# Gating's first projection as seven quarter products, with weight sums made in HBM and six token sums on GpSimd

## The chip, the cores and the metric

One core of a Trainium2 chip runs the kernel. The metric is the device time of one execution in microseconds (us). The engines are PE (TensorE, matmuls), DVE (VectorE), ACT (ScalarE), POOL (GpSimd) and SP (SyncE, which only issues transfers). Each runs its own instructions in order and waits on semaphores.

## The reference, cut to what matters

Two decoder layers on 512 tokens of width 1024. Layer 0 mixes tokens with a convolution module, layer 1 with spatial gating. After each comes a gated ConvFFN and, after every sublayer, a LayerNorm. The change lies in the gating of layer 1:

```python
z = gelu(x @ w_in + b_in)            # x 512 x 1024, w_in 1024 x 2048
u, v = split(z, 2)                   # 1024 columns each
v = layer_norm(v, ln_g, ln_b)
s = einsum("gts,bnsgc->bntgc", w_causal, v) + b_s   # 4 chunks of 128, 8 groups
y = (u * s) @ w_out + b_out
x = layer_norm(alpha * x + y)
```

All values are float32.

## The kernel before

**Numbers.** Each float32 operand is split into a high part (a copy in the matmul's float type, made by ACT) and a low part (the rest, a subtraction on DVE). A product is three matmuls: high by high, high by low, low by high.

**Weights.** All weights pass as units of 128 x 1024 (512 KB), numbered in order of use. SP loads unit u into slot u mod 4 of `raw` (L532) when the low part of unit u-4 is done (L560). `his` (L761) makes the high part, `los` (L1273) the low part, into rings of 4, some units ahead of PE. The first four units of the gating (U_GV to U_GV+3) go to places of their own, `eh` and `el`. `w_used` counts the units that PE is done with, and `his` waits for it before it overwrites a place.

**Order in time around the change.** The down-projection of the first ConvFFN (`ffn_down` on ACT and DVE, `ffn(0, 1, ...)` on PE) already works by Strassen's method with seven products. Its last one, `fourth` (L2342), ends token block by token block. Each block of 128 tokens is then normed on DVE (`mean_of`, `centred`, `normed`) and transposed on PE (`block_fm`, L2176) into PSUM. ACT copies it to `xh` (`block_hi`, L964), and DVE subtracts it to `xl` (`block_lo`, L1529).

**The v half** (L2388, L2389): `down_by_block(U_GV, ...)` makes columns 0 to 511 for one token block after the other, 24 matmuls each (L2027 to L2029), into banks 4 to 7; `down_by_k(U_GV + 4, ...)` makes columns 512 to 1023, unit by unit for all four blocks, into banks 0 to 3. DVE adds the bias row `gvrow` (L1943) into `vtm`, ACT takes Gelu (L1232), DVE takes statistics (L1948). `residual(2)` (L1544), which scales the residual and adds a bias row, stands on DVE between the two halves.

**The u half** (L2404 to L2413): 8 units, 24 matmuls each (`up`, L2012), each ending in a Gelu on ACT. Beside it DVE norms v (L1962, L1966), splits it and so feeds `spatial` (L2390), four groups of which follow the last two u units. `gated` (L1975) multiplies on DVE. Then the output projection (`down_by_k(U_GOUT, ...)`, L2421) needs `xl` of each group (L1996).

**GpSimd's queue**: for the first ConvFFN it makes the weight sums by transfers that add in HBM (`summed_weights`, L689), from raw copies that SP issues (`copies`, L534). Then come the roots of the norms (`norm_root`, L596), the mask of the spatial weights (L743) and the roots for v.

## Time and profile before

| | before |
|---|---|
| median of 3 runs | 1015.76 us (1015.53 to 1019.26) |
| profiled execution, its own time | 1015.58 us |
| its span, first to last instruction | 1013.8 us |
| share of the span: PE / DVE / ACT / POOL busy | 99% / 86% / 60% / 23% |
| the stage of the change, by PE | 525 to 618 us |

The page of the profile gives each engine's busy time and the groups of instructions. The timeline lists one engine's instructions with start, duration and line, and in brackets how long the engine was idle before it and what ended that. A matmul of 512 columns has a record of 0.39 us, but the next starts 0.23 us later: they are pipelined. The view of waits sums the idle time by what ended it. The view of stretches gives busy time and transfers between two moments.

### The profile page before, as it was taken

The page shows a single profiled execution, that of the slowest core. Times are in us where ns is not written, and L with a number is a line of the kernel's source. Part 1 is how long each engine was busy: PE and PEld are TensorE (multiplying, and loading weights), DVE is VectorE, ACT ScalarE, POOL GpSimd, SP SyncE. Part 2 cuts the span into 40 slices and gives each one's busy share as a digit, 9 for nine tenths or more (in the row PEclk, how much of TensorE's full clock was granted, in tenths as well). Part 3 has the DMA queues.
Part 4 walks back from the last instruction along what each step waited for, and adds up shares of the span by engine and source line. Part 5 has one row for each costly group of instructions (what it writes and reads, how often), then busy time and mean ns, then how long its engine had stood idle before and what let it go on. Part 6 is the DMA issues. An engine that isn't in the chain of part 4 may idle for free.

```text
span 1013.8 us, 15746 instructions
## 1 busy us (share of the span) xinstructions
PE 1003.6 (99%) x5379; PEld 861.1 (85%) x5379; DVE 867.6 (86%) x1228; ACT 604.5 (60%) x903; POOL 233.3 (23%) x289
## 2 busy tenths in 40 slices
PE   9999999999999999999999999999999999999997
PEld 7777788988899988888888888898988999888885
DVE  6999977897988988898894878779888888879888
ACT  7889865564565556666454343457555555566653
POOL 2998730023232121000010210002423212100001
PEclk9999999999999999999999999999999999999999
DMA  9766269369889676376555333825989966627652
GB/s 342 218 161 166 58 147 349 119 196 238 236 211 228 220 169 173 102 271 208 195 179 194 118 111 107 307 79 186 262 237 229 220 209 173 163 98 260 205 197 112
DMA packets 65590, 194.02 MB, mean 191 GB/s; under 512 B 7552, under 2 KB 8576, under 8 KB 65024
## 3 DMA queue, kind: packets, MB, share of 16 engines
q1 hardware_dynamic: 44144, 137.76, 39.1%
q0 software_dynamic: 19376, 48.24, 23.7%
q10 hardware_dynamic: 2016, 7.34, 2.1%
q8 instruction: 28, 0.46, 0.2%
q14 instruction: 26, 0.21, 0.1%
HBM read 178.11 MB, written 54.53 MB: 229 GB/s over the span
## 4 chain that ended last, share of the span: by engine, by line
PE 78%; DVE 5%; DMA 3%; issue 2%; ACT 1%; SPq 0%; DVEq 0%; POOL 0%; POOLq 0%; ACTq 0%
PE ps L2017 10%; PE ps L2018 10%; PE ps L2019 10%; PE ps L2306 6%; PE ps L2307 6%; PE ps L2308 6%; PE ps L2259 5%; PE ps L2260 5%; PE ps L2261 5%; PE ps L2027 4%; PE ps L2028 4%; PE ps L2029 4%; DMA raw<-d_weights 3%; PE ps L2186 1%; DVE ps L1618 1%
## 5 line engine op out<-in xcount | busy, mean ns | idle before, releaser
L2017 PE MATMUL ps<-xh,wh 128*128 128x512 f32 x528 | 208.5, 395 | 0.3 <-DVE wl L1280 0.3
L2018 PE MATMUL ps<-xl,wh 128*128 128x512 f32 x528 | 205.7, 390 | 0.0
L2019 PE MATMUL ps<-xh,wl 128*128 128x512 f32 x528 | 205.6, 389 | 0.0
L767 ACT ACTIVATE wh<-raw 128x1024 fp32r<-128x1024 f32 x114 | 119.9, 1057 | 80.4 <-PE ps L2308 49.5
L1280 DVE TENSOR_TENSOR wl<-raw,wh 128x1024 fp32r<-128x1024 f32 x101 | 123.2, 1224 | 32.9 <-ACT wh L767 32.5
L702 POOL DMA_DIRECT2D summed<-d_weights x88 | 75.2, 1115 | 198.0 <-PE ps L2019 96.4
L2017 PEld LDWEIGHTS ps<-xh,wh 128*128 128x128 f32 x528 | 99.2, 188 | 22.0 <-issue 1.2
L2019 PEld LDWEIGHTS ps<-xh,wl 128*128 128x128 f32 x528 | 99.1, 188 | 21.0
L2018 PEld LDWEIGHTS ps<-xl,wh 128*128 128x128 f32 x528 | 99.2, 188 | 20.7 <-issue 1.2
L2306 PE MATMUL ps<-wh,parts 128*128 128x512 f32 x264 | 102.9, 390 | 0.0
L2308 PE MATMUL ps<-wh,parts 128*128 128x512 f32 x264 | 102.7, 389 | 0.0
L2307 PE MATMUL ps<-wl,parts 128*128 128x512 f32 x264 | 102.7, 389 | 0.0
L1607 DVE TENSOR_TENSOR wl<-raw,wh 128x1024 fp32r<-128x1024 f32 x62 | 75.6, 1220 | 22.5 <-ACT wh L1014 22.5
L599 POOL TENSOR_SCALAR veps<-sqs 128x1 f32<-128x1 f32 x15 | 4.8, 323 | 385.2 <-ACT squares_down L961 266.2
L1376 DVE SCALAR_TENSOR_TENSOR ps<-glu,par,ps 128x512 f32<-128x512 f32 x125 | 84.7, 752 | 0.6 <-PE ps L2103 0.4
L622 POOL TENSOR_TENSOR gsum<-gsum,prods 128x512 f32<-128x512 f32 x53 | 70.2, 1324 | 14.5 <-ACT prods L836 8.4
L1014 ACT ACTIVATE wh<-raw 128x1024 fp32r<-128x1024 f32 x62 | 65.6, 1058 | 8.2 <-DMA raw<-d_weights 8.2
L1618 DVE SCALAR_TENSOR_TENSOR ps<-vpad,par,ps 128x512 f32<-128x512 f32 x80 | 60.3, 753 | 8.0 <-ACT ps L1038 2.2
L1618 DVE SCALAR_TENSOR_TENSOR ps<-gpad,par,ps 128x512 f32<-128x512 f32 x80 | 60.2, 753 | 6.4 <-DVE ps L1618 2.1
L2306 PEld LDWEIGHTS ps<-wh,parts 128*128 128x128 f32 x264 | 49.5, 188 | 11.1 <-DVE wl L1280 0.8
L2308 PEld LDWEIGHTS ps<-wh,parts 128*128 128x128 f32 x264 | 49.5, 188 | 10.4
L2307 PEld LDWEIGHTS ps<-wl,parts 128*128 128x128 f32 x264 | 49.6, 188 | 10.2
(266 smaller groups left out, 2543.9 us busy)
## 6 DMA issues: line engine op xcount, KB each, us to landing
raw<-d_weights SPq DMA_DIRECT2D x156, 512.0 KB, 4.9
raw<-summed SPq DMA_DIRECT2D x56, 512.0 KB, 4.1
summed<-d_weights POOLq DMA_DIRECT2D x88, 256.0 KB, 9.5
summed<-d_weights SPq DMA_DIRECT2D x66, 256.0 KB, 5.2
summed<-summed POOLq DMA_DIRECT2D x46, 256.0 KB, 4.8
res<-brow POOLq DMA_DIRECT2D x12, 512.0 KB, 10.7
wl<-raw POOLq DMA_DIRECT2D x4, 1024.0 KB, 6.9
wl<-raw POOLq DMA_DIRECT2D x5, 512.0 KB, 6.3
```

The lines of the kernel that those rows point to most:

```text
L702: eng.dma_start(out, of, accum_op=ALU.add).then_inc(w_sum[i % AHEAD], 16)
L767: eng.activation(split_at(u)[0], raw[:, u % RAW, :], ACT.Copy).then_inc(w_hi, 1)
L1280: eng.tensor_tensor(l, raw[:, u % RAW, :], h.bitcast(f32), ALU.subtract).then_inc(w_lo, 1)
L1376: eng.scalar_tensor_tensor(out=ps[:, bank, :], in0=glu[:, j % 2, k:k + SEQ], scalar=par[:, c:c + 1], in1=ps[:, bank, :], op0=ALU.mult, op1 ...
L1607: eng.tensor_tensor(wl[:, slot, :], raw[:, part, :], wh[:, slot, :].bitcast(f32), ALU.subtract).then_inc(w_lo, 1)
L1618: eng.scalar_tensor_tensor(out=accs[v], in0=buf[:, off:off + SEQ], scalar=par[:, bass.ds(cw, 1)], in1=accs[v], op0=ALU.mult, op1=ALU.add). ...
L2017: eng.matmul(ps[:, bank, cols], a, xh[:, k, cols], start=(k == 0), stop=False)
L2018: eng.matmul(ps[:, bank, cols], a, xl[:, k, cols], start=False, stop=False)
L2019: mm = eng.matmul(ps[:, bank, cols], b, xh[:, k, cols], start=False, stop=(k == KD - 1))
L2306: eng.matmul(ps[:, bank + t, :], s_h, w_h[:, cols], start=first, stop=False)
L2307: eng.matmul(ps[:, bank + t, :], s_h, w_l[:, cols], start=False, stop=False)
L2308: mm = eng.matmul(ps[:, bank + t, :], s_l, w_h[:, cols], start=False, stop=last)
```

## The change

The v half is made by Strassen's method (Winograd's form). The tokens and the input channels are cut in two each (A11, A12, A22 and so on), and so are the weights. Seven products of quarter size: P1 and P2 straight from x, a fourth (`g22`) with a weight sum, then one u unit (U_GU0), the fifth and sixth (`U_G56`), the third and seventh (`U_G37`), and the other seven u units. Six more units pass through the loads and the splits (GV_MORE).

- Weight sums: SP copies raw parts into `gsum_d` at units 22 to 25 of the first up-projection; GpSimd's queue adds to them behind `up_sums(0)`; SP waits for the sums before it loads U_GV+4.
- Token sums: ACT keeps copies of three token quarters (`block_kept`, `second_kept`), DVE makes `gn5` and `gs2`, GpSimd makes `gs4` and `gv7`, each for two token blocks. ACT and DVE split them (`token_hi`, `token_lo`).
- Outputs: DVE reads each product from PSUM and adds or subtracts it in `vtm`. GpSimd makes two of these sums (with `both_rows`, a sum of two bias rows, ahead).
- `residual(2)` moves behind the norm of v. Row transfers of ACT move.

The host puts the v weights into units whose halves are W11 | W21 and W12 | W22. The diff, cut:

```diff
+GQ = KD // 2
+U_GU0 = U_GV + GQ + 2
+U_G56 = U_GU0 + 1
+U_G37 = U_G56 + GQ
+U_GU = U_G37 + GQ - 1
 U_GOUT = U_GU + KD
+GV_MORE = 6
...
+        def gv_copies(i):
+
+            w1, w2 = weights_d[raw_gv + i], weights_d[raw_gv + GQ + i]
+            eng.dma_start(gsum_d[2 + i, :, 0:HALF], w1[:, 0:HALF]).then_inc(gv_copied, 16)
+            eng.dma_start(gsum_d[2 + GQ + i, :, HALF:UNIT], w2[:, 0:HALF]).then_inc(gv_copied, 16)
+            eng.dma_start(gsum_d[2 + GQ + i, :, 0:HALF], w2[:, HALF:UNIT]).then_inc(gv_copied, 16)
 
         for k in range(KD):
...
+                eng.wait_ge(gv_sum, 16 * (4 + 2 * GQ))
             load(u % RAW, u)
+            if 0 <= u - U_UP0 - 2 * KQ < GQ:
+                gv_copies(u - U_UP0 - 2 * KQ)
             for layer in range(DEPTH):
...
+        w1, w2 = weights_d[raw_gv:raw_gv + GQ], weights_d[raw_gv + GQ:raw_gv + 2 * GQ]
+        fifth, third = gsum_d[2:2 + GQ], gsum_d[2 + GQ:2 + 2 * GQ]
+        eng.wait_ge(gv_copied, 16 * 3 * GQ)
+        eng.dma_start(fifth[:, :, first], w2[:, :, first], accum_op=ALU.add).then_inc(gv_sum, 16)
+        eng.dma_start(third[:, :, second], w2[:, :, second], accum_op=ALU.add).then_inc(gv_sum, 16)
+        eng.wait_ge(gv_sum, 16 * 2)
+        eng.dma_start(fifth[:, :, second], fifth[:, :, first]).then_inc(gv_sum, 16)
+        eng.wait_ge(gv_sum, 16 * 3)
+        eng.dma_start(fifth[:, :, second], w2[:, :, second], accum_op=ALU.add).then_inc(gv_sum, 16)
+        eng.wait_ge(gv_sum, 16 * 4)
+        for i in range(GQ):
+            eng.dma_start(gsum_d[i // 2, :, second if i % 2 else first], fifth[i, :, second]).then_inc(gv_sum, 16)
+        eng.wait_ge(gv_sum, 16 * (4 + GQ))
+        for i in range(GQ):
+            eng.dma_start(gsum_d[i // 2, :, second if i % 2 else first], w1[i, :, second], accum_op=ALU.add).then_inc(gv_sum, 16)
         for t in range(NT):
             norm_root(ROOTS + NT + t, NT + t + 1, t)
+        eng.wait_ge(gv_in, 16)
+        eng.wait_ge(w_used, U_GV)
+        eng.tensor_tensor(both_rows[:, :], gvrow[:, 0:HALF], gvrow[:, HALF:D], ALU.add).then_inc(rows_ok, 1)
+        eng.wait_ge(rows_ok, 1)
+        for t in range(NT // 2):
+            eng.wait_ge(gv_rd, t + 1)
+            eng.tensor_tensor(vtm[:, 2 + t, HALF:D], vtm[:, 2 + t, 0:HALF], both_rows[:, :], ALU.subtract).then_inc(n_ok, 1)
+        eng.wait_ge(w_used, U_GV + GQ)
+        eng.wait_ge(x_kept, 2 * NT)
+        for t in range(NT // 2):
+            cols = slice(t * P, (t + 1) * P)
+            eng.wait_ge(ga_sum, 2 * t + 2)
+            eng.wait_ge(a22_kept, t + 1)
+            eng.tensor_tensor(gs4[:, :, cols], gs2[:, :, cols], a12f[:, :, cols], ALU.add).then_inc(ga_more, 1)
+            eng.tensor_tensor(gv7[:, :, cols], gs2[:, :, cols], a22f[:, :, cols], ALU.add).then_inc(ga_more, 1)
 
...
                 his([U_GV + 2, U_GV + 3])
+                block_kept(n, 0, 0)
+                block_kept(n, 0, 1)
...
+                his([U_GV + GQ, U_GV + GQ + 1])
                 squared(n, 3)
-                for t in (2, 3):
-                    block_hi(n, t, 0)
-                    block_hi(n, t, 1)
+                block_hi(n, 2, 0)
+                block_hi(n, 2, 1)
+                block_kept(n, 1, 0)
+                block_kept(n, 1, 1)
+                second_kept(0)
+                block_hi(n, 3, 0)
+                block_hi(n, 3, 1)
+                his([U_GU0])
+                second_kept(1)
 
         norm(0)
...
-                eng.activation(vtm[:, t, h * HALF:(h + 1) * HALF], vtm[:, t, h * HALF:(h + 1) * HALF], ACT.Gelu).then_inc(v_gelu, 1)
-                if h == 0:
-                    his([U_GV + 4 + t])
-            if h == 0:
-                row(glb[:, :], R_GLB, gm_in)
-                his(range(U_GU, U_GU + LEAD))
-        his([U_GU + LEAD])
+        token_hi(gn5h, gn5, 0, ga_sum, 1)
+        token_hi(gs2h, gs2, 0, ga_sum, 2)
+        his([U_G56])
+        token_hi(gn5h, gn5, 1, ga_sum, 3)
+        token_hi(gs2h, gs2, 1, ga_sum, 4)
+        his([U_G56 + 1])
+        gelu_v(0, 0, G_C11 - 1)
+        gelu_v(1, 0, G_C11)
+        row(glb[:, :], R_GLB, gm_in)
+        his([U_G56 + 2])
+        gelu_u(0)
+        his([U_G56 + 3])
+        for t in range(NT // 2):
+            token_hi(gs4h, gs4, t, ga_more, 2 * t + 1)
+            token_hi(gv7h, gv7, t, ga_more, 2 * t + 2)
+        his([U_G37, U_G37 + 1])
+        eng.wait_ge(w_used, U_G37)
+        row(glg[:, :], R_GLG, gm_in)
+        eng.dma_start(wsraw[:, :, :], spatial_d).then_inc(gm_in, 16)
+        his([U_G37 + 2, U_G37 + 3, unit_gu(1)])
+        gelu_v(0, 1, G_C12 - 1)
+        gelu_v(1, 1, G_C12)
+        his([unit_gu(2)])
+        for h, last in ((1, G_C22), (0, G_C21)):
+            for t in range(NT // 2):
+                gelu_v(2 + t, h, last - 1 + t)
+        his([unit_gu(3), unit_gu(4)])
         eng.wait_ge(ws_m, 1)
...
+
+        def gv_first(t):
+
+            eng.wait_ge(gv_pe, t + 1)
+            eng.tensor_tensor(vtm[:, 2 + t, 0:HALF], ps[:, 4 + t, :], gvrow[:, 0:HALF], ALU.add).then_inc(gv_rd, 1)
...
             normed(n, 3)
+            gv_first(1)
             block_lo(n, 2)
+            los([U_GV + GQ, U_GV + GQ + 1])
             block_lo(n, 3)
 
         first_halves(0, U_CONV_OUT + 4)
...
 
-        eng.wait_ge(gv_in, 16)
-        for h in range(2):
-            for t in range(NT):
-                if h == 0 and t < NT - 1:
-                    eng.wait_ge(blk, blk_gv + t + 1)
-                else:
-                    eng.wait_ge(w_used, U_GV + 4 * (h + 1))
-                cols = slice(h * HALF, (h + 1) * HALF)
-                eng.tensor_tensor(vtm[:, t, cols], ps[:, 4 - 4 * h + t, :], gvrow[:, cols], ALU.add).then_inc(v_ev, 1)
-                if h == 0:
...
-            if h == 0:
-                los([U_GU])
-                residual(2)
-                los([U_GU + 1, U_GU + 2])
-        los([U_GU + LEAD])
+        def token_lo(to, of, high, t, count):
+
+            cols = slice(t * P, (t + 1) * P)
+            eng.wait_ge(ga_hi, count)
+            eng.tensor_tensor(to[:, :, cols], of[:, :, cols], high[:, :, cols].bitcast(f32), ALU.subtract).then_inc(ga_lo, 1)
+
+        def gv_stat(t, h, count):
+
+            eng.wait_ge(v_gelu, count)
+            return stat(eng.bn_stats(stats[:, t, h, :], vtm[:, t, h * HALF:(h + 1) * HALF]))
...
+        eng.wait_ge(w_used, U_GV + GQ)
+        for t in halves:
+            eng.wait_ge(gv_rd, t + 1)
+            eng.tensor_tensor(vtm[:, t, c1], ps[:, 6 + t, :], vtm[:, 2 + t, c1], ALU.add).then_inc(gv_rd, 1)
+        los([U_GU0])
+        eng.wait_ge(x_kept, 2 * NT)
+        for t in halves:
+            cols = slice(t * P, (t + 1) * P)
+            eng.wait_ge(a22_kept, t + 1)
+            eng.tensor_tensor(gn5[:, :, cols], ps[:, B0[1] + 2 * t, :].rearrange("p (k n) -> p k n", k=4), a22f[:, :, cols],
+                              ALU.subtract).then_inc(ga_sum, 1)
+            eng.wait_ge(ga_sum, 2 * t + 1)
+            eng.tensor_tensor(gs2[:, :, cols], gn5[:, :, cols], a11f[:, :, cols], ALU.subtract).then_inc(ga_sum, 1)
+        eng.wait_ge(ga_sum, 4)
+        token_lo(gn5l, gn5, gn5h, 0, 1)
+        token_lo(gs2l, gs2, gs2h, 0, 2)
+        los([U_G56])
+        los([U_G56 + 1])
+        token_lo(gn5l, gn5, gn5h, 1, 3)
+        token_lo(gs2l, gs2, gs2h, 1, 4)
+        los([U_G56 + 2])
+        eng.wait_ge(w_used, U_GU0)
+        eng.wait_ge(n_ok, NT // 2)
+        for t in halves:
+            eng.tensor_tensor(vtm[:, 2 + t, c1], ps[:, 4 + t, :], vtm[:, 2 + t, c1], ALU.add).then_inc(gv_rd, 1)
+        los([U_G56 + 3])
+        for t in halves:
+            token_lo(gs4l, gs4, gs4h, t, 4 + 2 * t + 1)
+            token_lo(gv7l, gv7, gv7h, t, 4 + 2 * t + 2)
+        los([U_G37, U_G37 + 1])
+        eng.wait_ge(w_used, U_G37)
+        for t in halves:
+            eng.wait_ge(gv_rd, G_MP4)
+            eng.tensor_tensor(vtm[:, 2 + t, c1], ps[:, 2 + t, :], vtm[:, 2 + t, c1], ALU.add).then_inc(gv_rd, 1)
+        for t in halves:
+            eng.tensor_tensor(vtm[:, 2 + t, c2], ps[:, 2 + t, :], vtm[:, 2 + t, c2], ALU.add).then_inc(gv_rd, 1)
+        los([U_G37 + 2, U_G37 + 3])
+        for t in halves:
+            eng.wait_ge(gv_rd, G_NP6 - 1 + t)
+            eng.tensor_tensor(vtm[:, 2 + t, c2], vtm[:, 2 + t, c2], ps[:, t, :], ALU.subtract).then_inc(gv_rd, 1)
+        gv_stat(0, 0, 1)
+        gv_stat(1, 0, 2)
+        los([unit_gu(1)])
+        eng.wait_ge(gv_pe, 3)
+        for t in halves:
+            eng.wait_ge(gv_rd, G_NP5 - 1 + t)
+            eng.tensor_tensor(vtm[:, t, c2], ps[:, 6 + t, :], vtm[:, 2 + t, c2], ALU.subtract).then_inc(gv_rd, 1)
+        eng.wait_ge(w_used, U_GU + 1)
+        for t in halves:
+            eng.wait_ge(gv_rd, G_C12 - 1 + t)
+            eng.tensor_tensor(vtm[:, 2 + t, c2], ps[:, 4 + t, :], vtm[:, 2 + t, c2], ALU.subtract).then_inc(gv_rd, 1)
+        for t in halves:
+            eng.tensor_tensor(vtm[:, 2 + t, c1], vtm[:, 2 + t, c1], ps[:, 4 + t, :], ALU.subtract).then_inc(gv_rd, 1)
+        los([unit_gu(2)])
+        gv_stat(0, 1, 3)
+        gv_stat(1, 1, 4)
+        gv_stat(2, 1, 5)
+        gv_stat(3, 1, 6)
+        gv_stat(2, 0, 7)
+        n = gv_stat(3, 0, 8)
+        los([unit_gu(3)])
         eng.wait_ge(st_ok, n)
...
+
+        residual(2)
 
         def gated(g):
...
-                block_fm(1, 2 + t)
-        down_by_block(U_GV, 4, 4, xh, xl, 0, KD, last_block, lambda t: wait_x(1, t))
-        down_by_k(U_GV + 4, 4, 0, xh, xl, 0, KD)
+        g11, g12, g22 = [[x[:, k, t] for x in (xh, xl)] for k, t in
+                         ((slice(0, GQ), slice(0, HQ)), (slice(GQ, KD), slice(0, HQ)), (slice(GQ, KD), slice(HQ, SEQ)))]
+        gn5p, gs2p, gs4p, gv7p = (gn5h, gn5l), (gs2h, gs2l), (gs4h, gs4l), (gv7h, gv7l)
+
+        def gv(u, c, bank, tokens, i, t):
+
+            h, l = split_at(u)
+            w_h, w_l = h[:, c * HALF:(c + 1) * HALF], l[:, c * HALF:(c + 1) * HALF]
+            s_h, s_l = [x[:, i, t * P:(t + 1) * P] for x in tokens]
+            eng.matmul(ps[:, bank + t, :], s_h, w_h, start=(i == 0), stop=False)
+            eng.matmul(ps[:, bank + t, :], s_h, w_l, start=False, stop=False)
+            return eng.matmul(ps[:, bank + t, :], s_l, w_h, start=False, stop=(i == GQ - 1))
+
+        for t in range(NT // 2):
+            wait_x(1, t)
+            for i in range(GQ):
+                if t == 0:
+                    eng.wait_ge(*lo_of(U_GV + i))
+                mm = gv(U_GV + i, 0, 4, g11, i, t)
+            mm.then_inc(gv_pe, 1)
+            eng.wait_ge(c_rd, R_P4 + 1 + t)
+            for i in range(GQ):
+                mm = gv(U_GV + i, 1, 6, g12, i, t)
+                if t == 1:
+                    mm.then_inc(w_used, 1)
+            block_fm(1, 2 + t)
+        eng.wait_ge(gv_rd, G_M)
+        for t in range(NT // 2):
+            wait_x(1, 2 + t)
+            for i in range(GQ):
+                u = U_GV + GQ + i // 2
+                if t == 0 and i % 2 == 0:
+                    eng.wait_ge(*lo_of(u))
+                mm = gv(u, i % 2, 4, g22, i, t)
+                if t == 1 and i % 2:
+                    mm.then_inc(w_used, 1)
+        eng.wait_ge(*lo_of(U_GU0))
+        eng.wait_ge(gv_rd, G_C11)
+        up(split_at(U_GU0), GU_BANK[0]).then_inc(w_used, 1)
+        for pair in range(GQ // 2):
+            for t in range(NT // 2):
+                eng.wait_ge(ga_lo, 2 * t + 2)
+                for i in (2 * pair, 2 * pair + 1):
+                    u = U_G56 + i
+                    if t == 0:
+                        eng.wait_ge(*lo_of(u))
+                    gv(u, 0, 0, gn5p, i, t)
+                    mm = gv(u, 1, 2, gs2p, i, t)
+                    if t == 1:
+                        mm.then_inc(w_used, 1)
+
+        def gv_third(i):
+            eng.wait_ge(*lo_of(U_G37 + i))
+            for t in range(NT // 2):
+                mm = gv(U_G37 + i, 0, 6, gs4p, i, t)
+            if i == GQ - 1:
+                mm.then_inc(gv_pe, 1)
+
+        def gv_seventh(i):
+            for t in range(NT // 2):
+                mm = gv(U_G37 + i, 1, 4, gv7p, i, t)
+            mm.then_inc(w_used, 1)
+
+        eng.wait_ge(ga_lo, 8)
+        eng.wait_ge(u_gelu, 1)
+        eng.wait_ge(gv_rd, G_MP4)
+        for i in range(GQ):
+            gv_third(i)
+            if i < GQ - 2:
+                gv_seventh(i)
+        gv_seventh(GQ - 2)
+        gv_seventh(GQ - 1)
 
         def spatial(g):
...
 
-        for j in range(KD):
+        for j in range(1, KD):
             eng.wait_ge(*lo_of(U_GU + j))
-            if j < 4:
-                eng.wait_ge(v_ev, j + 1)
-            else:
-                eng.wait_ge(u_gelu, j - 3)
-            up(split_at(U_GU + j), 4 + j % 4).then_inc(w_used, 1)
+            if j == 1:
+                eng.wait_ge(gv_rd, G_NP5)
+            if j == 5:
+                eng.wait_ge(gv_rd, G_C21)
+            up(split_at(U_GU + j), GU_BANK[j]).then_inc(w_used, 1)
             if j >= KD - 2:
...
     weights = np.ascontiguousarray(np.concatenate(units))
 
```

## Rows read from the trace of the kernel before

**Rows 1.** The page, part 1: busy us (share of the span) xinstructions.

```profile
PE 1003.6 (99%) x5379; PEld 861.1 (85%) x5379; DVE 867.6 (86%) x1228; ACT 604.5 (60%) x903; POOL 233.3 (23%) x289
```

**Rows 2.** Waits of PE, whole span: us in total, times, longest.

```profile
PE ps L2146 <- POOL ident L606: 1.6, 1, 1.6
PE ps L2259 <- DVE wl L1684: 0.8, 1, 0.8
```

**Rows 3.** Timeline of PE: start us, us, engine, line, operation.

```profile
525.06 0.48 PE L2027 MATMUL ps<-eh,xh 128*128 128x512 f32 x1
...
537.90 0.47 PE L2027 MATMUL ps<-eh,xh 128*128 128x512 f32 x1
...
570.64 0.39 PE L2017 MATMUL ps<-xh,wh 128*128 128x512 f32 x1
...
617.84 0.45 PE L2027 MATMUL ps<-wh,xh 128*128 128x512 f32 x1
```

**Rows 4.** Stretches: us, busy us (instructions) per engine, granted clock, DMA share, GB/s.

```profile
525.06:570.64 45.58, 45.58 (x211) 37.71 (x210) 29.95 (x36) 16.21 (x22) 4.16 (x5) 1.00 0.55 187
```

**Rows 5.** Groups by line: operation, shapes, count, busy us, mean ns, idle before.

```profile
L767 ACT ACTIVATE wh<-raw 128x1024 fp32r<-128x1024 f32 x114 | 119.9, 1057 | 80.4 <-PE ps L2308 49.5
L1280 DVE TENSOR_TENSOR wl<-raw,wh 128x1024 fp32r<-128x1024 f32 x101 | 123.2, 1224 | 32.9 <-ACT wh L767 32.5
L1376 DVE SCALAR_TENSOR_TENSOR ps<-glu,par,ps 128x512 f32<-128x512 f32 x125 | 84.7, 752 | 0.6 <-PE ps L2103 0.4
L622 POOL TENSOR_TENSOR gsum<-gsum,prods 128x512 f32<-128x512 f32 x53 | 70.2, 1324 | 14.5 <-ACT prods L836 8.4
...
L1800 DVE TENSOR_TENSOR parts<-made,parts 128x512 fp32r<-128x512 f32 x50 | 32.5, 687 | 0.0
```

**Rows 6.** Timelines of DVE and POOL, 527 to 536 us.

```profile
527.03 1.22 DVE L1280 TENSOR_TENSOR el<-raw,eh 128x1024 fp32r<-128x1024 f32 x1
...
533.79 1.29 DVE L1772 SCALAR_TENSOR_TENSOR res<-scaled_down,rstd,brow_n 128x1024 f32<-128x1024 f32 x1 [0.89 <-POOL rstd L588]
534.99 1.28 DVE L1532 TENSOR_TENSOR xl<-ps,xh 128x512 fp32r<-128x512 f32 x2
...
533.14 0.54 POOL L588 TENSOR_TENSOR rstd<-veps,half_m 128x1 f32<-128x1 f32 x1
```

**Rows 7.** DVE beside POOL: timelines, and L1548's durations (min/median/max ns).

```profile
559.55 1.68 POOL L743 TENSOR_SCALAR_AFFINE_SELECT wsraw<-wsraw 128x1024 f32<-128x1024 f32 x1 [25.87 <-DMA glb<-d_rows]
...
L1548 DVE SCALAR_TENSOR_TENSOR res<-res,brow x4: 1214/1214/2124, 560.2 to 564.5; 128x1024 f32<-128x1024 f32 x4
...
106.11 7.01 POOL L622 TENSOR_TENSOR gsum<-gsum,prods 128x512 f32<-128x512 f32 x5 [2.08 <-ACT prods L836]
...
112.44 1.24 DVE L1321 TENSOR_TENSOR glul<-glu,gluh 128x512 fp32r<-128x512 f32 x1
...
580.90 1.22 DVE L1280 TENSOR_TENSOR wl<-raw,wh 128x1024 fp32r<-128x1024 f32 x1
...
581.38 0.81 POOL L593 TENSOR_SCALAR veps<-mv 128x1 f32<-128x1 f32 x1
```

**Rows 8.** Timeline of DVE, 577 to 614 us.

```profile
577.90 1.27 DVE L1962 SCALAR_TENSOR_TENSOR vtm<-vtm,mv,glg 128x1024 f32<-128x1024 f32 x1
...
597.86 1.23 DVE L1970 TENSOR_TENSOR vl<-vtm,vh 128x1024 fp32r<-128x1024 f32 x1
...
609.79 0.69 DVE L1982 TENSOR_TENSOR vtm<-ps,bsrow 128x512 f32<-128x512 f32 x1 [3.34 <-PE ps L2401]
...
613.92 1.22 DVE L1280 TENSOR_TENSOR wl<-raw,wh 128x1024 fp32r<-128x1024 f32 x1
```

**Rows 9.** Transfers: a stretch, ACT's timeline, ACT's waits between 150 and 250 us.

```profile
290.00:300.00 10.00, 10.00 (x51) 8.51 (x51) 8.81 (x14) 5.19 (x9) 2.46 (x3) 1.00 1.06 261
...
289.51 1.06 ACT L1014 ACTIVATE wh<-raw 128x1024 fp32r<-128x1024 f32 x1 [1.88 <-DMA raw<-d_weights]
...
ACT wh L1014 <- DMA raw<-d_weights: 4.5, 1, 4.5
```

100 lines of the change are left out of this document (67 added, 33 removed).

## Prediction

> **What bounds the kernel now.** I read the page first: TensorE (PE) is busy for 99% of the span [rows 1]. Then the waits of PE: the longest anywhere is 1.6 us, and there is none in the stage that is changed [rows 2]. So today every microsecond of matmul work is on the path, and work of the other engines costs only when it makes PE wait. Next the timeline of PE in the stage. The first projection (the v half) starts at 525.06, its third token block at 537.90, the other half (u) at 570.64, and the output projection at 617.84 [rows 3]. Between 537.90 and 570.64 lie 2 x 24 + 4 x 24 = 144 matmuls, so one takes 32.74 / 144 = 0.227 us. Last, the stretch 525.06 to 570.64 by engine: VectorE (DVE) is busy for 30.0 of 45.6 us, ScalarE (ACT) for 16.2, GpSimd (POOL) for 4.2, PE's granted clock is 1.00 [rows 4]. DVE has 15.6 us free there. I take the change to be a trade: less work on PE for more on DVE and POOL, and ask at each step what is late.
>
> **Removed.** Strassen computes the v half with seven quarter products in place of eight: 7 x 24 = 168 matmuls for 192. 24 x 0.227 = **-5.4 us**, and since PE waits for nothing here, all of it counts until another engine is late.
>
> **Added, by count.** Six more weight units, each with a load, a high part on ACT (1.06 us) and a low part on DVE (1.22 us) [rows 5]: 7.3 us of DVE. Eight low parts of token sums and four token sums, each 512 columns at 0.69 [rows 5]: 8.3. Eighteen readings of products where eight were: ten more, 6.9. Together 22.5 us of DVE, for 15.6 free. Part of it goes behind the u units, and `residual(2)` (about 5 us) leaves the stretch. So DVE is full rather than over-full, and the order inside decides. POOL gets seven sums of 1.32 us [rows 5]. ACT gets 6 x 1.06 plus some 14 pieces of 0.6: 15 us, for 29 free; it is nowhere last, and its three row transfers and its Gelu table load lie before waits for DVE. Each order below is walked with these durations; an instruction of 512 columns holds DVE for 0.60, one of 1024 for 1.14 to 1.20, since neighbours overlap a little [rows 6].
>
> **Step A: the first products eat units twice as fast.** P1 takes three matmuls from a unit where a block took six, so it wants the low part of unit U_GV+3 after 9 matmuls: 525.06 + 9 x 0.227 = 527.1. DVE makes it from 527.03 to 528.25, behind two steps of the norm [rows 6]. Before, it was wanted only after 18 matmuls, at 529.1. Nothing in the change moves it. **+1.1 us**, and I hold this for the surest cost. The order then runs to the fourth product at 537.90 + 1.1 = 539.0.
>
> **Step B: GpSimd's first three sums.** Both a VectorE instruction with two SBUF inputs and a GpSimd one seem to need something that only one can have. At 560.2 one of four equal `residual` instructions took 2.12 us where the median is 1.21, beside GpSimd's mask at 559.55 to 561.23. At 112.44 a 512-column subtraction took 1.24 in place of 0.69, beside the last of five GpSimd sums, which ended at 113.12. DVE goes on 0.13 before the GpSimd record ends, in both [rows 7]. The other way, a GpSimd instruction asked at 581.38 and ended at 582.19, right after DVE's 580.90 + 1.22: it slips in between two back-to-back DVE instructions [rows 7]. So I let the two engines take turns, and a GpSimd sum costs a DVE instruction of that kind up to 1.19 us. `both_rows` has no open wait after the root that ends about 533.7, where DVE starts the last `normed` at 533.79 [rows 6]: DVE waits 1.2. One of the next two sums falls beside readings of PSUM, which are free; the other delays the low part of U_GV+4 by 0.7. Add `gv_first` (0.60). The low part ends at 539.8 or so, against 539.0 plus its own hand-over: **+1.0 us**. If GpSimd comes after `normed`, U_GV+5 is late instead, by 0.8.
>
> The Trainium skill, page "SBUF — State Buffer", section "Who interferes with whom", says that a VectorE instruction with two SBUF inputs contends with a GpSimd one that reads SBUF and that the loser is blocked for the whole instruction. By that rule each turn costs 1.32 and not 1.19, and the time below would be 0.8 us more. That it holds at all speaks against giving sums to GpSimd; these rows agree but for the last 0.13.
>
> **Step C: the token sums.** Behind the fourth product's units DVE has two readings, one low part, and then `gn5`, `gs2` twice. The first `gs2` ends at 545.7, and GpSimd starts its four sums at once. The next four DVE instructions with two SBUF inputs (`gs2`, `token_lo` twice, the low part of U_G56) each find it taken: 0.6 + 1.1 + 1.2 + 1.2 = 4.1 us. The low part of U_G56 is done at 553.5. PE has finished u unit 0, put there as a cover, at 539.0 + 1.0 + 48 x 0.227 = 550.7. **+2.9 us.** Without the turns it would be done near 548 and the cover would be enough. After that DVE keeps 0.5 to 2 us ahead to the end of the seventh product, though each unit's low part is wanted every 1.4 to 2.7 us.
>
> **Step D: behind the product.** Four readings, a low part, six statistics and another low part follow PE's last matmul: the norm of v starts 8.8 us after it. Today 577.90 - 570.64 = 7.3. The norm takes 597.86 - 577.90 = 20.0 [rows 8] and 1.1 for its last piece. Before, 3.3 us of idle lay ahead of `gated(0)` and more before that [rows 8]. Now `residual(2)` stands there: 4 x 1.20 = 4.8. Then two low parts 2.3, `gated(0)` and `gated(1)` 613.92 - 609.79 = 4.1, a low part 1.1, the first `xl` 0.7. Sum 8.8 + 20.0 + 1.1 + 4.8 + 2.3 + 4.1 + 1.1 + 0.7 = 42.9. PE needs 7 x 24 x 0.227 = 38.1 and 4 spatial groups of 0.9: 41.7. **+1.2 us.** Were `residual(2)` free, PE would be last.
>
> **Step E: transfers.** Twelve copies of 256 KB stand on SP's queue in the first up-projection, and GpSimd issues sums of 1 MB parts after `up_sums(0)`, far ahead of their use (about 100 us). The loads behind the copies land later. ACT waited 1.9 us for one at 289.51 and up to 4.5 us for one earlier, with no wait of PE beside either [rows 9, 2]. I put this at **0**, hidden by the three units that the split runs ahead; the bounds are in the rivals. It could not be below nothing.
>
> **Sum.** -5.4 + 1.1 + 1.0 + 2.9 + 1.2 = +0.8. The profiled execution took 1015.58 us (span 1013.8), within 0.2 of the median of 1015.76. 1015.6 + 0.8 = **1016.4 us**.
>
> **Rivals.**
> 1. The turns do not happen, or GpSimd waits instead of DVE. For: the small GpSimd instruction at 581.38 waited for DVE, not the other way [rows 7], and DVE's 125 taps, with one SBUF input, kept 752 ns beside GpSimd's sums [rows 5]. Against: the two rows of step B, both of this very kind. B and C fall: 1015.6 - 5.4 + 1.1 + 1.2 = 1012.5.
> 2. Slower, by step E. Place: units 22 to 25 of the first up-projection, near 284 to 306 us, where the DMA engines are fully busy (1.06) at 261 GB/s [rows 9]. Price: 0.75 MB per unit is 2.9 us at that rate, 5.7 if read and write both count. It decides from where ACT's wait passes the 4.5 us that stayed hidden: 1.9 + 2.9 = 4.8 is just there, 1.9 + 5.7 = 7.6 costs 3.1 a unit. Two units with such a delay give 1016.4 + 6 = 1022.6; all four 1029. Against: the same copies for the first 11 units cost PE nothing.
> 3. The change does not save its matmuls' time, PE being held at DVE's pace all through: 22.5 us more on DVE with 15.6 free is 6.9 over, less 5 moved away, less 5.4 saved, leaves DVE's idle time of start and end as the only reserve. That gives 1016 to 1018, inside the range.
>
> **Chances.** Forecast with its variants (1014.5 to 1018.5) 0.62; rival 1 0.19; rival 2 0.11; something beyond 0.08. Range: 1012.0 to 1019.0, from rival 1 to the forecast with every turn whole and 2 us of step E. A measurement of this kernel can tell about 0.5%, 5.1 us. The saving is 5.4 at most, and step A alone eats 1.1, so faster by more than that is hardly possible: 0.03. Slower needs 1020.8 or more: 0.11. Same: 0.86.
>
> **What would show it.** In PE's waits: about 1.1 us for the low part of `el` at the first product (A); about 1 us near 539 (B); 2 to 3 us for the first unit of the fifth product near 551 (C); about 1 us at the output projection for `xl` (D). In DVE's timeline: `token_lo` and low parts of 1.3 to 2.4 us beside GpSimd's sums. If all DVE instructions there keep 0.69 and 1.22, rival 1 holds. If PE waits before 420 us, rival 2 does. A new wait elsewhere, above all for a raw unit or for ACT, would make the prediction wrong.

## The result, and the profile after

The changed kernel takes 1033.76 us (median of 4 runs, 1032.52 to 1039.21), the kernel before 1016.29 in the same comparison. The ratio is 1.018, with a 95% interval of 1.014 to 1.022: slower by about 17 us, where the prediction said no change. The profiled execution took 1032.52 us, with a span of 1030.8.

The page of the changed kernel, part 1, against [rows 1]:

```profile
PE 1002.9 (97%) x5355; PEld 859.2 (83%) x5355; DVE 891.8 (87%) x1256; ACT 617.3 (60%) x923; POOL 253.8 (25%) x308
```

There are 24 matmuls fewer, as the change says. But PE is busy for 97% of the span now, not 99%. Its waits, over the whole span, against [rows 2] (us in total, times, longest):

```profile
PE ps L2443 <- ACT made L1153: 6.9, 2, 5.8
PE ps L2577 <- DVE wl L1401: 2.9, 2, 2.5
PE ps L2443 <- DVE wl L1805: 1.8, 1, 1.8
...
PE ps L2490 <- DVE wl L1401: 1.1, 2, 0.6
PE ps L2577 <- DVE el L1401: 0.9, 1, 0.9
PE ps L2212 <- DVE xl L2181: 0.7, 1, 0.7
```

Two places are to be told apart. L2577 and L2212 are matmuls of the gating stage and of its output projection: the waits of steps A to D. L2443 is in the first up-projection, some 220 us earlier, where no matmul was changed. That is the larger part. The timeline of PE, first at the up-projection and then in the stage (start, us, operation, and in brackets the idle time before it with what ended it):

```profile
308.09 0.39 PE L2443 MATMUL ps<-parts,wh 128*128 128x256 f32 x1 [1.81 <-DVE wl L1805]
310.89 0.39 PE L2443 MATMUL ps<-parts,sum2h 128*128 128x256 f32 x1 [1.10 <-ACT made L1153]
319.75 0.58 PE L2443 MATMUL ps<-xh,parts 128*128 128x256 f32 x1 [5.78 <-ACT made L1153]
...
543.05 0.50 PE L2577 MATMUL ps<-eh,xh 128*128 128x512 f32 x1 [0.92 <-DVE el L1401]
554.41 0.47 PE L2577 MATMUL ps<-wh,xh 128*128 128x512 f32 x1 [0.41 <-DVE wl L1401]
...
632.69 0.47 PE L2212 MATMUL ps<-wh,xh 128*128 128x512 f32 x1 [0.69 <-DVE xl L2181]
```

**Where the 17 us are.** I cut both executions at five matmuls of PE: the first of the first up-projection (`fh`), the first of the down-projection (`wh,parts`), the first of the gating stage (`eh`), the last of the gating output projection (`bh`), and the last of all. The differences of their starts, in us:

| execution | to up | up | down | gating stage | second layer | end | span |
|---|---|---|---|---|---|---|---|
| before | 182.6 | 235.4 | 107.1 | 141.7 | 339.9 | 7.2 | 1013.8 |
| after | 184.9 | 245.9 | 109.1 | 141.8 | 339.8 | 9.3 | 1030.8 |
| difference | +2.3 | +10.5 | +2.0 | +0.1 | 0 | +2.1 | +17.0 |

"End" is from the start of the last matmul to the end of the span. The stage that the change is about came out even: +0.1, where the prediction had +0.8. All the rest lies outside it. The first column differs among all the executions of this study by up to 2.7 us without a pattern. Besides the 1.6 us of [rows 2], PE waits there for 1.3 us for `xh` and 1.2 for `res` in after, but for 0.4 us in all in e4 and 2.3 in e5 (both below), which run the same instructions there as after; so the +2.3 is not put down to the change. The up-projection of the eleven kernels that have none of the copies in it, or only one of them, takes from 234.0 to 236.0 (234.7 in the mean), so differences under 2 us between two executions are not read there.

**The up-projection.** In SP's queue, each of the four loads (L571) is followed by three copies (L584 to L586), and the loads after them come late. SP's timeline at the fourth of them, and ACT's (start, us):

```profile
292.26 0.60 SPq L571 DMA_DIRECT2D raw<-d_weights  x1
292.91 1.40 SPq L584 DMA_DIRECT2D gsum<-d_weights  x1
294.35 3.06 SPq L585 DMA_DIRECT2D gsum<-d_weights  x1
297.45 0.61 SPq L586 DMA_DIRECT2D gsum<-d_weights  x1
...
318.37 1.06 ACT L1101 ACTIVATE wh<-raw 128x1024 fp32r<-128x1024 f32 x1 [6.93 <-DMA raw<-d_weights]
325.43 1.06 ACT L1101 ACTIVATE wh<-raw 128x1024 fp32r<-128x1024 f32 x1 [5.46 <-DMA raw<-d_weights]
```

ACT waits for raw weights, its next instruction (`made`) stands behind that wait, and PE waits for `made`. Of the transfers issued from 250 to 300 us (KB each, median us to landing), the copies take three times as long as the loads:

```profile
raw<-d_weights SPq DMA_DIRECT2D x8, 512.0 KB, 6.4
gsum<-d_weights SPq DMA_DIRECT2D x12, 256.0 KB, 18.9
```

The median hides what happens to the four loads. The first of them, and the fourth, issued at 292.26:

```profile
raw<-d_weights SPq DMA_DIRECT2D x1, 512.0 KB, 5.5
...
raw<-d_weights SPq DMA_DIRECT2D x1, 512.0 KB, 26.0
```

The two between them took 11.1 and 18.8 us: each load, with three copies more ahead of it, takes 5.6 to 7.7 us longer to land than the one before. The fourth lands at 318.3, and with it ACT's wait of 6.93 us ends. In the kernel before the loads issued from 280 to 292 us land after 6.6 to 9.3 us.

And PE does not run at full clock when it comes back. Stretches (length, then busy us and instructions of PE, PEld, DVE, ACT, POOL, then granted clock, DMA share, GB/s):

```profile
315.00:320.00 5.00, 0.25 (x1) 0.25 (x2) 0.54 (x1) 1.60 (x3) 0.81 (x1) 0.80 1.08 250
320.00:325.00 5.00, 5.00 (x25) 5.00 (x26) 1.08 (x2) 0.00 (x0) 0.00 (x0) 0.52 1.06 340
```

PE is busy for 0.25 us from 315 to 320 us, and then works for 5 us at 0.52 of the full clock, the level of 1.2 GHz: some 2.4 us lost (0.48 of 5 us). Waits of 8.7 us, what each hides besides (below, 0.7), 2.4 for the clock, less the 0.8 and 0.2 of before's own wait at this line [rows 2]: 10.8 for 10.5 measured.

### The profile page after: what moved, and what is told of

Same layout as the page of the kernel before. It is cut to its first block, busy times and chain, and to the rows that moved or that the text cites. A ratio compares the mean times of both kernels' runs of the same rounds, so it can differ in the third digit from the quotient of the medians.

```text
span 1030.8 us, 15810 instructions
## 1 busy us (share of the span) xinstructions
PE 1002.9 (97%) x5355; PEld 859.2 (83%) x5355; DVE 891.8 (87%) x1256; ACT 617.3 (60%) x923; POOL 253.8 (25%) x308
## 4 chain that ended last, share of the span: by engine, by line
PE 44%; DVE 7%; issue 2%; DMA 2%; ACT 1%; POOL 0%; DVEq 0%; POOLq 0%; ACTq 0%
PE ps L2202 5%; PE ps L2203 5%; PE ps L2204 5%; PE ps L2490 4%; PE ps L2491 4%; PE ps L2492 4%; PE ps L2444 3%; PE ps L2445 3%; PE ps L2443 3%; DVE wl L1401 2%; PE ps L2212 1%; PE ps L2213 1%; PE ps L2214 1%; DMA raw<-d_weights 1%; DMA raw<-summed 1%
## 5 line engine op out<-in xcount | busy, mean ns | idle before, releaser
L847 ACT ACTIVATE wh<-raw 128x1024 fp32r<-128x1024 f32 x120 | 125.7, 1056 | 84.0 <-PE ps L2492 41.2
L1401 DVE TENSOR_TENSOR wl<-raw,wh 128x1024 fp32r<-128x1024 f32 x107 | 132.3, 1245 | 22.8 <-ACT wh L847 21.8
L1728 DVE TENSOR_TENSOR wl<-raw,wh 128x1024 fp32r<-128x1024 f32 x62 | 75.6, 1220 | 27.1 <-ACT wh L1101 27.0
L1101 ACT ACTIVATE wh<-raw 128x1024 fp32r<-128x1024 f32 x62 | 65.5, 1057 | 21.0 <-DMA raw<-d_weights 21.0
## 6 DMA issues: line engine op xcount, KB each, us to landing
res<-brow POOLq DMA_DIRECT2D x12, 512.0 KB, 10.8
```

The lines of the kernel that those rows point to most:

```text
L847: eng.activation(split_at(u)[0], raw[:, u % RAW, :], ACT.Copy).then_inc(w_hi, 1)
L1401: eng.tensor_tensor(l, raw[:, u % RAW, :], h.bitcast(f32), ALU.subtract).then_inc(w_lo, 1)
L1728: eng.tensor_tensor(wl[:, slot, :], raw[:, part, :], wh[:, slot, :].bitcast(f32), ALU.subtract).then_inc(w_lo, 1)
```

## What a wait costs beside what is listed

The stage's sum needs one more number. Around the longest wait in the stage (PE, timeline of after):

```profile
565.19 0.39 PE L2204 MATMUL ps<-xh,wl 128*128 128x512 f32 x1
568.09 0.47 PE L2577 MATMUL ps<-wh,gn5h 128*128 128x512 f32 x1 [2.52 <-DVE wl L1401]
568.40 0.39 PE L2578 MATMUL ps<-wl,gn5h 128*128 128x512 f32 x1
```

A matmul is listed with 0.39 us though the next one starts 0.227 later. Idle time is counted from the listed end. So from 565.19 to 568.09 PE lost 2.90 - 0.227 = 2.67, not 2.52; and the first matmul after the wait holds the next back by 0.31, not 0.227. This wait costs 0.16 + 0.08 = **0.24 us more than the view lists**. As an estimate I take the same for the other three. With it the stage adds up: -24 x 0.227 = -5.45, waits 0.92 + 0.41 + 2.52 + 0.69 = 4.54, four times 0.24 = 0.96; sum +0.05, measured +0.1. A check by the starts of matmuls: from the first product to the fourth it is 12.84 us in before and 14.58 in after, so 1.74 us for the first two waits, where the estimate has 1.81.

## The experiments

Times are medians; "before" is the kernel before in the same comparison, on the same chip.

**1. Are the transfers what costs, and which?** Four kernels. *e1* keeps the changed stage and leaves out every transfer that makes the sums (the ten summed units are loaded from raw weights, so the v half works on wrong weights). *e2* is the kernel before with the twelve copies alone, in SP's queue where the change has them (GpSimd waits for them behind `up_sums(0)`). *e3* is the changed kernel with the copies one per load at units 32 to 43. *e4* is the changed kernel with the copies issued by GpSimd, at step 20 of its sums of the first layer.

```diff
# e1
-            if 0 <= u - U_UP0 - 2 * KQ < GQ:
-                gv_copies(u - U_UP0 - 2 * KQ)
-        eng.dma_start(fifth[:, :, first], w2[:, :, first], accum_op=ALU.add).then_inc(gv_sum, 16)
...
-            return gsum_d[u - U_GV - GQ]
+            return weights_d[raw_gv + u - U_GV]
# e3
-            if 0 <= u - U_UP0 - 2 * KQ < GQ:
-                gv_copies(u - U_UP0 - 2 * KQ)
+            if 0 <= u - U_UP0 - 32 < 3 * GQ:
+                gv_copy(u - U_UP0 - 32)
# e4, in GpSimd's summed_weights
+                if layer == 0 and step == 20:
+                    for n in range(3 * GQ):
+                        gv_copy(n)
```

> The changed kernel without any of the transfers that make the gating's weight sums (no copies, no adding transfers, no wait for them); the ten summed units are loaded from the raw weights instead, so the sums, and with them the output of the gating, are not computed. Theory 1 (the copies delay the loads of the first up-projection): PE's waits of 1.8 and 6.9 us between 300 and 320 us are gone, the changed stage keeps its four waits (4.6 us), and the time is that of the kernel before within 2 us: 1015 to 1018. Rival (the loss is due to the six more units, VectorE's load and the moved orders): the time stays above 1028.

> The kernel before with nothing but the twelve copies added on SP's queue at units 22 to 25 of the first up-projection. Theory 1: PE waits 7 to 9 us between 300 and 320 us as in the changed kernel, and the time rises by 9 to 14 us, to 1025 to 1030. If the adding transfers of GpSimd's queue carry the loss instead: under 1018. Together with the first run this splits the loss into copies and adding transfers.

> The changed kernel with the same twelve copies, one behind each of the loads 32 to 43 of the first up-projection in place of three behind each of 22 to 25. Theory 1: the waits near 310 us are gone; the DMA engines are less busy there (0.6 to 0.8 of their time against 1.06), so a single copy of 256 KB costs a load 1 to 2 us, which stays hidden: 1015 to 1019. If the amount of transfers counts and not the place: 1028 or more.

> The changed kernel with the same twelve copies at about the same time, but issued from GpSimd's queue, between its own adding transfers. Theory 1a (loads stand behind the copies in SP's queue, in order): the loads pass them, PE waits under 2 us near 310, time 1016 to 1022. Theory 1b (the DMA engines are full there and everything slows, whoever issues): PE waits stay at 5 us or more, time 1025 to 1035; GpSimd's own sums then run later too.

| kernel | time | ratio to before (95%) | up | down | stage | end |
|---|---|---|---|---|---|---|
| e1 no transfers | 1016.94 | 1.0022 (1.0012 to 1.0031) | 235.4 | 107.2 | 143.5 | 7.2 |
| e2 before + copies | 1028.67 | 1.0133 (1.0116 to 1.0150) | 248.2 | 107.2 | 141.7 | 7.2 |
| e3 copies spread | 1022.23 | 1.0059 (1.0037 to 1.0082) | 236.5 | 108.9 | 143.5 | 9.3 |
| e4 copies from GpSimd | 1022.99 | 1.0084 (1.0068 to 1.0101) | 235.8 | 107.6 | 143.4 | 9.3 |

Before was 1014.83. e2 alone brings 13.8 us to a kernel whose gating stage is untouched: the copies are the cause of the up-projection's loss. It is 12.8 us there, for 10.5 in after, with the same 8.7 us of waits: the granted clock is 0.50 in two stretches of 5 us (from 310 and from 320 us), where after has one. The waits of e2:

```profile
PE ps L2273 <- ACT made L1080: 5.5, 2, 4.6
PE ps L2273 <- DVE wl L1698: 3.2, 1, 3.2
```

e4 moves the same bytes at nearly the same time (its twelve issues run from 280.06 to 286.3 us, after's from 284.0 to 298.1), and the up-projection is back at 235.8. Six kernels with the copies on that queue have 235.1 to 236.2, 235.8 in the mean, against 234.7 without: about 1 us, not 11 to 13. The landings say on whom the delay falls. In after GpSimd's row additions (`res<-brow`) land after 14.1 us, as in before (14.0), and SP's loads after up to 26.0. In e4 SP's loads of this place land after 8 to 10 us, about as in before, and the row additions, now behind the copies, after 18.5. So what costs is not the bytes but their place ahead of the loads in SP's queue. Two things limit this. e4 changes more than the queue: its copies start 4 us earlier and go ahead of the row additions. And e3, whose copies stay ahead of loads in SP's queue, one per load from 332 us on, waits for 0.9 us only; the seven copies issued before 370 us land after 6.3 (median). The place costs where the copies stack up. With e4 ACT waits up to 4.4 us for raw weights from 250 to 360 us, and PE 1.3 us in the whole projection:

```profile
ACT wh L1103 <- DMA raw<-d_weights: 12.8, 5, 4.4
...
gsum<-d_weights POOLq DMA_DIRECT2D x12, 256.0 KB, 9.4
```

The Trainium skill, page "DMA: Bandwidth & Descriptors", section "Queues, rings and completion order", says that a DMA engine takes turns between the queues it has work for, and takes one queue's descriptors in their order. The landings of after and e4 agree: in SP's own queue the copies hold the loads back, from another they share with them.

e1, e3 and e4 have a longer stage than after has, 143.4 to 143.5 for 141.8, with the same waits (0.92 to 0.93, 0.41 to 0.46, 2.52 to 2.54, 0.68 to 0.69). The granted clock tells why. From 554 to 558 us, behind the 2.5 us wait, in e1; and 568 to 572, the same place, in after:

```profile
554.00:558.00 4.00, 3.68 (x10) 2.96 (x11) 4.00 (x6) 3.26 (x6) 0.00 (x0) 0.62 0.73 232
...
568.00:572.00 4.00, 3.91 (x17) 3.30 (x18) 4.00 (x6) 3.15 (x5) 0.00 (x0) 1.00 0.64 203
```

Ten matmuls start in the 4 us instead of 17. In e4 and e3 the clock of the same place is 0.61 (554 to 558 and 558 to 562). The same wait of 2.5 us cost 1.6 us more in three of four profiled executions, through the clock. What decides whether it falls is not shown.

**2. Step C: do GpSimd's sums hold DVE?** The rows of after first, DVE and POOL from 560 us:

```profile
560.89 1.44 DVE L2090 TENSOR_TENSOR gs<-gn,a11f 128x512 f32<-128x512 f32 x1
562.37 1.67 DVE L2069 TENSOR_TENSOR gn5l<-gn,gn5h 128x512 fp32r<-128x512 f32 x1
563.96 1.77 DVE L2069 TENSOR_TENSOR gs2l<-gs,gs2h 128x512 fp32r<-128x512 f32 x1
565.66 3.42 DVE L1401 TENSOR_TENSOR wl<-raw,wh 128x1024 fp32r<-128x1024 f32 x2
...
560.49 1.29 POOL L819 TENSOR_TENSOR gs<-gs,a12f 128x512 f32<-128x512 f32 x1 [7.30 <-DVE gs L2090]
561.75 1.74 POOL L820 TENSOR_TENSOR gv<-gs,a22f 128x512 f32<-128x512 f32 x1
563.45 1.74 POOL L819 TENSOR_TENSOR gs<-gs,a12f 128x512 f32<-128x512 f32 x1
565.14 1.72 POOL L820 TENSOR_TENSOR gv<-gs,a22f 128x512 f32<-128x512 f32 x1
```

Instructions of 0.69 us take 1.44 to 1.77, two low parts of 2.35 take 3.42. GpSimd's own take 1.74 where the free one took 1.29. *e5* is e1 with GpSimd writing a constant in place of each of its four token sums (its other two sums are of outputs), so `gs4` and `gv7` aren't computed. *e6* is e4, complete, with the sums held back.

```diff
# e5, on e1
-            eng.tensor_tensor(gs4[:, :, cols], gs2[:, :, cols], a12f[:, :, cols], ALU.add).then_inc(ga_more, 1)
-            eng.tensor_tensor(gv7[:, :, cols], gs2[:, :, cols], a22f[:, :, cols], ALU.add).then_inc(ga_more, 1)
+            eng.memset(gs4[:, :, cols], 0.0).then_inc(ga_more, 1)
+            eng.memset(gv7[:, :, cols], 0.0).then_inc(ga_more, 1)
# e6, on e4, ahead of GpSimd's four sums
+        eng.wait_ge(ga_lo, 4)
```

> This is the kernel of the run without the gating sums (the ten summed units loaded from raw weights, the sums themselves left out), with one more change: GpSimd's four token sums (gs4 and gv7, 128x512 each, out of two SBUF operands) are replaced by four writes of a constant, which read nothing. Every wait and signal stays. The fifth and seventh... products therefore work on wrong tokens; the number of matmuls is the same. Theory of step C (turns): in the run without the sums DVE's seven instructions beside GpSimd's four took 0.16 + 0.39 + 0.49 + 1.07 = 2.1 us more than the same forms alone, and PE waited 2.5 us at the first matmul of the fifth product. Without the sums that wait should fall to 0.0 to 0.6 us, and with it the restart (0.2 to 0.3 us) and the lowered clock behind it (0.62 in 554 to 558 us, about 1.7 us of lengthened matmuls): 3.5 to 4.5 us less, so 1012.5 to 1013.5 us against 1016.9. Rival (DVE simply has too much to do between the two products, or ACT's high parts come late): DVE's forms were never what was late, the wait stays at 1.5 us or more and the time moves by under 1.5 us. Second rival: a constant's write takes the same turns as a sum; then DVE's instructions beside it stay at 1.67 to 1.77 us for a token low part and nothing changes.

> The kernel with the twelve copies on GpSimd's queue, complete, and GpSimd's four token sums held back until DVE has made the four low parts of the fifth product's tokens (one more wait, for ga_lo at 4). Theory of step C: the turns move from the chain that PE waits for to DVE's low parts of the weight units 3 and 4 of the fifth product, which have 4 to 9 us to spare (a unit there is 12 matmuls of 0.389 us, so unit 2 is wanted 9.3 us after the first). The wait at the first matmul of the fifth product falls from 2.5 to under 0.6 us, the clock there stays at 1.00, and the third and seventh products begin without a wait. 3.5 to 4.5 us less than with the copies on GpSimd's queue alone (1022.99): 1018.5 to 1019.5 us. Rival: GpSimd's sums, now ending about 7 us later, are late for ACT's high parts and DVE's low parts of gs4 and gv7, and PE waits instead at the first matmul of the next product; then the time falls by less than 2 us or rises.

e5 takes 1012.51 us, before 1014.87: ratio 0.9973 (0.9960 to 0.9985), and 4.4 less than e1. The four writes take 0.53 us each, DVE keeps 0.69 beside them, and PE does not wait at the fifth product:

```profile
545.42 0.53 POOL L800 MEMSET gs<- 128x512 f32 x1 [7.27 <-DVE gs L2071]
...
546.57 0.69 DVE L2050 TENSOR_TENSOR gn5l<-gn,gn5h 128x512 fp32r<-128x512 f32 x1
...
550.38 0.39 PE L2558 MATMUL ps<-wh,gn5h 128*128 128x512 f32 x1
```

The stage is 139.1 us long, 2.6 under before, with the waits of steps A, B and D left in it. Theory C is shown: the sums' reading is what held DVE. e6 takes 1018.69 us (ratio 1.0040, 1.0026 to 1.0054), 4.3 less than e4, stage 140.1. In one point it missed: the first two low parts of `gs4` and `gv7` took their turns now (1.77 us each, the last two 0.68), and PE waited for 0.8 us at the first matmul of the next product. The end of the span did not move (9.3).

**3. Steps A and D: two moves in DVE's order.** *e7* is e6 with both.

```diff
             mean_of(n, 2)
-            centred(n, 2)
             los([U_GV + 3])
+            centred(n, 2)
...
         los([U_G37, U_G37 + 1])
+        residual(2, range(2))
         eng.wait_ge(w_used, U_G37)
...
+        residual(2, range(2, 4))
         eng.wait_ge(w_used, U_GU + 1)
...
-        residual(2)
```

> As the run before it (copies on GpSimd's queue, sums held back), and two moves in DVE's order. Step A: the low part of the fourth unit of the first product stands before centred(2) instead of behind it. Step D: residual(2) is taken from between the normalisation of v and the gate, and its four instructions of 1.16 us are put by twos into DVE's two idle stretches of the stage, of 2.45 and 1.42 us, ahead of the waits for the fifth and for the second product's banks. Theory: the waits of 0.9 (el) and 0.7 us (xl) go, with a restart of 0.2 to 0.3 us each; the stage is then 24 x 0.227 = 5.4 us shorter than before, less what is left at 539 us (0.45 and a restart): 4.5 us shorter than in the kernel before. The gain is about 2 us against the run before it: 1016.5 to 1017.5 us. Against before it stays 1 to 3 us slower, by what the transfers cost elsewhere. Rival: residual(2) in the gaps makes DVE late for the next product's bank (0.9 us over the second gap), and the 2 us come back as a wait there: 1018 to 1019 us.

It took 1021.95 us, 3.3 more than e6, and the stage 141.8, 1.7 more. The waits for `el` and `xl` are gone, and others stand in their place (the second of these was there in e6, 0.80):

```profile
544.56 0.47 PE L2580 MATMUL ps<-wh,xh 128*128 128x512 f32 x1 [1.45 <-DVE wl L1404]
567.41 0.47 PE L2580 MATMUL ps<-wh,gs4h 128*128 128x512 f32 x1 [0.82 <-DVE wl L1404]
574.89 0.50 PE L2580 MATMUL ps<-wh,gs4h 128*128 128x512 f32 x1 [1.77 <-DVE wl L1404]
586.54 0.50 PE L2205 MATMUL ps<-xh,wh 128*128 128x512 f32 x1 [0.47 <-DVE wl L1404]
```

The first one answers to 542.26 of e6, where it was 0.42: DVE has no free time from the first product to the fourth, so PE, let go 0.9 earlier, waits 1.0 longer there. The move of step A buys nothing. The third and fourth are the rival of the expectation: `residual(2)` in DVE's gaps makes the next low parts late. The idle gap was DVE's lead over the products, not spare time.

**4. What do the transfers cost outside the up-projection?** *e8* is the kernel before with all 24 transfers, from GpSimd's queue, their results unused. *e9* has the twelve copies only. *e10* is e6 with the eight last transfers merged into four of 512 KB.

```diff
# e10
-        for i in range(GQ):
-            eng.dma_start(gsum_d[i // 2, :, second if i % 2 else first], fifth[i, :, second]).then_inc(gv_sum, 16)
+        for b, half_of in enumerate((first, second)):
+            eng.dma_start(gsum_d[0:GQ // 2, :, half_of], fifth[b::2, :, second]).then_inc(gv_sum, 16)
```

> The kernel before, with every transfer that makes the gating sums (the twelve copies, from GpSimd's queue, and the adding transfers behind up_sums), whose results nobody loads. It tells what the making of the sums costs by itself. Theory: three places, read off the run with the copies on GpSimd's queue: 0.5 us in the up-projection, 0.4 us in the down-projection and 2.2 us between the last matmul and the end of the span: 1014.8 + 3.1 = 1018 us, and the gating stage keeps its 141.2 us. Rival: the 2.2 us at the end come from the changed kernel's own instructions (its code, its order, its semaphores) and not from the transfers; then the end takes 7.6 us as in before, and the time is 1015.5 to 1016 us.

> The kernel before and the twelve plain copies from GpSimd's queue, without the adding transfers behind up_sums; the copies' results are loaded by nobody. In the kernel before with all of the transfers the time from the last matmul to the end of the span was 9.4 us instead of 7.2. If the adding transfers cause that (their number on GpSimd's software queue, or their bytes), the end is 7.2 us again, the down-projection keeps before's length and the time is 1015.5 to 1016.5 us. Rival: any twelve more transfers on GpSimd's queue lengthen the end; then it is 9.3 us and the time 1017.5 to 1018.5 us.

> The complete kernel with the copies on GpSimd's queue and its token sums held back, and the eight last transfers of the sums (four copies, four adding ones, 256 KB each) merged into two and two of 512 KB, so that the adding stage issues eight transfers instead of twelve; bytes are the same. If the longer end goes by the number of transfers it falls from 9.3 to about 8.5 us; if it goes by bytes, packets or by there being any, it stays 9.3. The down-projection should change by under 0.5 us. Time 1018 to 1019 us (1018.69 without the merging), about 3.5 us above before: the stage is 1.6 us shorter than before's, and the transfers cost 4 to 5 us elsewhere.

| kernel | time | before | ratio (95%) | down | stage | end |
|---|---|---|---|---|---|---|
| e8 | 1020.35 | 1014.87 | 1.0051 (1.0034 to 1.0068) | 108.4 | 141.7 | 9.4 |
| e9 | 1019.67 | 1015.15 | 1.0044 (1.0029 to 1.0058) | 107.1 | 141.8 | 9.8 |
| e10 | 1024.80 | 1015.15 | 1.0089 (1.0075 to 1.0103) | 114.9 | 140.2 | 9.3 |

Two things. The adding transfers run in the down-projection and cost 0.4 to 2.6 us there (107.1 before; 109.1 in after, 107.6 in e4, 108.4 in e8, 109.7 in e7); without them (e9) it is 107.1. And the end is longer by 2.1 to 2.6 us in all three, with adding transfers or without: the rival of e9's expectation held. Both times came out above what even the nearer expectation said, e8 by 2.3 us and e9 by 1.2. e10 was a plain mistake. Its transfers issued from 435 to 500 us, and under them those of e6:

```profile
q0 software_dynamic: 5930, 2.07, 17.0%
...
gsum<-d_weights POOLq DMA_DIRECT2D x2, 512.0 KB, 26.1
```

```profile
gsum<-d_weights POOLq DMA_DIRECT2D x4, 256.0 KB, 11.6
```

The same 2 MB went in 5930 packets, for 916 in e6, and the adding half took 26 us to land, and PE waited in the down-projection for 5.8 us in all. The merged ones differ from the others in their outermost dimension, 2 units where it was 128 rows; that this is the cause is likely and was not tried by itself. The packets are smaller too (0.35 KB for 2.3 in the mean), and the run doesn't part the two. The Trainium skill, page "DMA: Bandwidth & Descriptors", section "Why a DMA increments its semaphore by 16 and not by 1", says that a transfer is dealt to the largest number of engines up to 16 that divides the slowest dimension of both its sides: that would be 2 engines of 16. No view of these runs shows engines singly. An estimate from the rows speaks for it and proves nothing: two transfers at a time on 2 engines each, for 17.2 us (the plain pair) and 26.1, would be 10.8 us of all 16 engines, and the queue's 17.0% of 65 us are 11.0.

**5. The end of the span.** SP's last output transfer is issued 4.8 us after the last matmul in before and 4.7 in after. What follows is 2.4 us in before (1011.42 to 1013.8) and 4.6 in after (1026.19 to 1030.8). The last two transfers land 2.0 us after their issue in both; in the rest, 0.4 and 2.6 us, the trace shows nothing. Seven kernels, all the kernel before with one thing more on GpSimd's queue:

```diff
# e11: gv_copy(0) alone, 256 KB, signals gv_copied (new)      # e12: the same, one row of 2 KB
# e15: e12 without GpSimd's wait for gv_copied                # e16: e12's transfer behind the row additions
# e13: no transfer more, one semaphore more
-                eng.dma_start(res[:, t, :], brow[:, :], accum_op=ALU.add).then_inc(res_add, 16)
+                eng.dma_start(res[:, t, :], brow[:, :], accum_op=ALU.add).then_inc(res_add if t < NT - 1 else res_last, 16)
# e14: a transfer more, no semaphore more
+            if layer == 0:
+                eng.dma_start(spare_d[:, 0:HALF], weights_d[0, 0:1, 0:HALF]).then_inc(res_add, 16)
# e17: e14 with a new semaphore
-                eng.dma_start(spare_d[:, 0:HALF], weights_d[0, 0:1, 0:HALF]).then_inc(res_add, 16)
+                eng.dma_start(spare_d[:, 0:HALF], weights_d[0, 0:1, 0:HALF]).then_inc(spare_ok, 16)
```

> The kernel before and one plain copy of 256 KB on GpSimd's queue, in place of the twelve; its result is loaded by nobody. It asks how the longer end of the span (7.2 us from the last matmul to the end in before, 9.3 to 9.8 us in every kernel with more transfers on GpSimd's queue, whether twelve copies, twelve adding ones or both) goes with their number. If by number or bytes, one copy of twelve gives 7.4 us and a time of 1015.3 us; if it is there as soon as there is one more (a threshold), 9.3 us and 1017.5 us.

> As the run with one copy, but the copy is of one row of 2 KB instead of 128 (256 KB). If the 2.6 us at the end of the span go with there being one more transfer on GpSimd's queue, whatever its size, the end stays at 9.3 to 9.8 us and the time at 1017.4 us; if they go with the bytes or packets that the queue has moved, the end is 7.2 us and the time 1015 us.

> The kernel before with no transfer more, but the fourth transfer of each of GpSimd's row additions (res += brow) signals a semaphore of its own, so that its queue uses one semaphore more; the two places that wait for the additions wait for both. If the 2.1 to 2.6 us at the end of the span go with the number of semaphores that GpSimd's queue signals, the end from the last matmul is 9.3 to 9.8 us here and the time about 1017.4 us; if with a transfer more, it is 7.2 us and the time that of before, 1014.8 us.

> The kernel before with one transfer more on GpSimd's queue (one row of 2 KB), which signals a semaphore that this queue used already. If the end goes with semaphores, it is 7.2 us from the last matmul and the time 1014.8 us; if with transfers, 9.3 to 9.8 us and 1017.4 us.

> The run with one row of 2 KB at step 20, without GpSimd's wait for it; nothing waits for that transfer. If the wait of GpSimd for a semaphore of its own queue that no other transfer signals brings the longer end, it is 7.2 us from the last matmul here; if the transfer's place or its semaphore brings it, 9.3 to 9.8 us.

> The same transfer with the same new semaphore and GpSimd's wait behind up_sums, but issued right behind the four row additions, where the run with one more transfer on a used semaphore has it. If the place at step 20 brings the longer end, it is 7.2 us here; if the new semaphore with a transfer more does, 9.3 to 9.8 us.

> The kernel before with one transfer more on GpSimd's queue (one row of 2 KB into a small tensor), which signals a semaphore that nothing else signals; ACT waits for it. The same with a used semaphore cost nothing (1014.69). If the pair of transfer and new semaphore brings the longer end, it is 9.3 to 9.8 us from the last matmul and the time 1017.4 us; if the tensor of ten units as destination does, it is 7.2 us and 1014.8 us.

| kernel | more transfers | new semaphore | time | before | end |
|---|---|---|---|---|---|
| e11 | 1 of 256 KB | yes | 1017.44 | 1015.14 | 9.8 |
| e12 | 1 of 2 KB | yes | 1017.76 | 1014.35 | 9.8 |
| e13 | none | yes | 1014.94 | 1014.75 | 7.2 |
| e14 | 1 of 2 KB | no | 1014.69 | 1014.75 | 7.2 |
| e15 | 1 of 2 KB, waited for by none | yes | 1018.56 | 1015.06 | 9.8 |
| e16 | 1 of 2 KB, other place | yes | 1017.93 | 1015.06 | 9.6 |
| e17 | 1 of 2 KB, small tensor | yes | 1017.55 | 1014.86 | 9.6 |

It is neither bytes nor place nor a wait: e14 and e17 differ in the semaphore that one transfer of 2 KB signals and that ACT waits for, and in 2.9 us (ratios 0.9999, 0.9989 to 1.0008, and 1.0025, 1.0015 to 1.0035). e13 shows that the semaphore alone costs nothing. In these runs only a transfer more together with a semaphore more on that queue brings it, and e2, whose copies signal a new semaphore from SP's queue, has an end of 7.2 us. The last transfer and the span's end in both, DMA issues of SP:

```profile
1010.52 0.33 SPq L581 DMA_DIRECT2D d_out<-res  x1
```

```profile
1011.42 0.33 SPq L582 DMA_DIRECT2D d_out<-res  x1
```

The first is e14, with a span of 1012.9; the second e17, with 1016.2: 2.4 and 4.8 us. What happens in that time, beyond the 2.0 us of the landing, isn't shown.

**6. The best complete kernel.** *e18* is e6 with all 24 transfers issued by GpSimd behind `up_sums(0)`, signalling `w_sum[0]`, which that queue uses already, in place of `gv_copied` and `gv_sum`.

```diff
-        eng.wait_ge(gv_copied, 16 * 3 * GQ)
-        eng.dma_start(fifth[:, :, first], w2[:, :, first], accum_op=ALU.add).then_inc(gv_sum, 16)
+        def gv_issue(out, of, **how):
+            issued[0] += 16
+            eng.dma_start(out, of, **how).then_inc(w_sum[0], 16)
...
+        gv_issue(fifth[:, :, first], w2[:, :, first], accum_op=ALU.add)
```

> The complete changed kernel with GpSimd's token sums held back, all 24 transfers of the sums issued by GpSimd behind up_sums, and signalling a semaphore of that queue that is used already instead of two new ones. Theory: the end of the span is 7.2 us again, 2.1 us less than in the run with the sums held back (1018.69); the up-projection is free of the copies (0.3 us less), the down-projection keeps 1 to 2 us of waits: 1016 to 1017 us, which is still over before's 1015. Rival: the tensor of the sums as destination brings the longer end; then it stays 9.3 us and the time 1018.5 to 1019 us.

It took 1016.85 us, before 1014.86: ratio 1.0014 (1.0005 to 1.0023). The end is 7.2 us again, up 234.0, stage 140.2, and down 110.0, where all the copying now lies. That is 17 us better than the change as it was made, and still 2 us behind the kernel before.

## Why the prediction was wrong

**Removed**: right. 24 matmuls less at 0.227.

**Step A**: predicted +1.1, measured 0.92 listed and 0.24 beside it, 1.16. Right in place and size.

**Step B**: predicted +1.0; 0.41 + 0.24 = 0.65. The turn was there: the last `normed` took 2.24 us beside `both_rows` in place of 1.28. I had it at 1.19 and got 0.96, and the second turn was shorter as well.

**Step C**: predicted +2.9, by turns of DVE with GpSimd; 2.52 + 0.24 = 2.76. Right, and e5 shows the mechanism. (The prediction's own terms, 539.0 + 1.0 + 48 x 0.227, give 550.9 and not 550.7, so +2.6; the miss was small either way.) It left out that a wait this long can lower the clock (1.6 us more in e1, e3 and e4).

**Step D**: predicted +1.2; 0.69 + 0.24 = 0.93. The norm of v began 8.8 us after the last matmul of the product, as said.

The stage's four terms sum to 5.5 where the prediction had 6.2, so the stage came out at +0.1 for +0.8. All four mechanisms stand. The error is elsewhere.

**Step E** failed: "I put this at 0, hidden by the three units that the split runs ahead". The transfers cost 10.5 us in the up-projection (e2 shows that the copies alone bring it), 2.0 in the down-projection and 2.1 at the end. Three things were wrong in it.

1. The cover was named and not counted: no row showed how late a load may land before PE waits. From 250 to 360 us ACT's waits for raw units and raw parts sum to (longest in brackets) 7.2 us (1.9) in before, 12.3 (4.5) in e1, 15.6 (4.4) in e4, 19.3 (3.8) in e3, 27.9 (7.8) in e2 and 28.5 (6.9) in after. PE's waits in the up-projection are 0.8, 0.7, 1.3, 0.9, 8.7 and 8.7. So up to a longest wait of 4.5 us, or a sum of 19, PE lost about a microsecond, and beyond it 8.7; the runs don't tell whether the longest or the sum decides.
2. Rival 2 had the right place, and its higher price, 5.7 us a unit, was near what the loads behind each further three copies show (5.6 to 7.7 us later to landing). But by bytes over bandwidth e4 should pay the same, and it pays about 1 us: the price is of order in a queue. The rival gave 1022.6 or 1029, for 1033.8 measured; the lowered clock (2.4 us) and the end of the span (2.1) were in neither.
3. What spoke against rival 2 was "the same copies for the first 11 units cost PE nothing". Seven of those groups were issued from 151 to 172 us in before, where the DMA share is 0.99 to 1.05 as well, and their loads landed after 4.9 to 11.0 us. So a full DMA share [rows 9] doesn't tell the two places apart. What differs near 290 us is what else is in flight: GpSimd's row additions and adding transfers (14 us to landing), where its queue issues nothing from 144 to 182 us, and 250 to 270 GB/s are moved, for up to 395. No run takes these away, so their part isn't shown; but the row to weigh was what the other queue does in each place, and the rival should have had more than the 0.11 that I gave.

**The chances.** "Slower" had 0.11 and was the case. **Rival 1**, that the turns don't happen, gave 1012.5: e5, which takes the four token sums' turns away, has 1012.51, but with the late `xl` and `el` as predicted and without the transfers; the agreement to the digit is chance. **Rival 3**, DVE as the bound all through, is half right. DVE is busy for 48.2 of 50.0 us in the v half now (30.0 of 45.6 in [rows 4]), and e7 shows that from the first product to the fourth a wait removed comes back as another.

## What to carry to other kernels

Work that is moved into "free" transfers is to be costed by what stands behind it in its own queue, not by its bytes: the same twelve copies cost 13 us when they stacked up ahead of loads in one queue, and about 1 us from another queue or one per load. "Hidden" needs a row that shows the lead of the very loads that are held back; the DMA share doesn't tell, it was at 1 where copies were free and where they were not. And an engine's idle time between two waits is often its lead: before filling it, look at who is waiting for what comes after.

## What was not expected of the hardware

- One transfer more on GpSimd's queue, when it signals a semaphore that nothing else on it signals, lengthens the end of the span by 2.4 to 2.6 us (e11, e12, e15 to e17); the same transfer on a used semaphore by nothing (e14). The cause is open.
- The listed idle time before a matmul of 512 columns is too short, by 0.24 us at the wait of 2.52: 0.16 in the listed end of the matmul before, 0.08 in the one behind.
- After a wait of 2.5 us the granted clock was 0.61 to 0.62 for some 4 us in three of four executions (1.6 us lost), and 1.00 in the fourth.
- A write of a constant on GpSimd (0.53 us for 128x512) doesn't slow DVE's instructions with two SBUF inputs; a sum (1.29) does, and is itself lengthened to 1.74.
- Two adding transfers of 512 KB with an outermost dimension of 2 took 26.1 us to land, four of 256 KB with the same bytes and 128 rows outermost 11.6.
- Copies that stack up in one queue delay the loads of that queue (5.5, 11.1, 18.8 and 26.0 us to landing), while the row additions of the other queue land after 14.1 us as before.
